# Latent attention with its score blocks in reverse order and a softmax handed over in three parts

## The reference

```
q = rmsnorm(c_q) @ w_q_b          # 128 plain + 64 rotary columns a head
kv = rmsnorm(c_kv) @ w_kv_b       # 128 key + 128 value columns a head
sc = (q_nope . k_nope + q_rope . k_rope) * 192 ** -0.5
p  = softmax(where(key_pos <= q_pos, sc, -1e30))    # blocks of 128 queries
y  = p @ v
```

## Time and profile before

| | |
|---|---|
| median of 3 runs | 2827.41 us (2825.73 to 2827.95) |
| profiled execution | 2832.14 us |
| its span | 2830.3 us, mean granted clock of TensorE 0.988 |
| TensorE busy | 2750.7 us, 97% of the span |
| VectorE / ScalarE / GpSimd busy | 1307.0 / 999.7 / 1069.2 us |

### The profile page before, as it was taken

How to read it: one execution, slowest core, us unless ns; L and a number is a source line. 1 busy time by engine, 2 the same in 40 slices (tenths; PEclk the granted TensorE clock), 3 DMA queues, 4 the chain that set the end, 5 groups by cost and what they waited for, 6 DMA issues and landing times.

```text
span 2830.3 us, 33382 instructions
## 1 busy us (share of the span) xinstructions
PE 2750.7 (97%) x13100; PEld 2283.2 (81%) x13100; DVE 1307.0 (46%) x1887; ACT 999.7 (35%) x1566; POOL 1069.2 (38%) x528
## 2 busy tenths in 40 slices
PE   8999998899999999889999999999999999999997
PEld 7888887788888888777878888888878888888886
DVE  6466647823255665683334555453343222222323
ACT  5235435423224443453342333233223333333221
POOL 1443332244444333223443333333434444444442
PEclk9999998999999999999999999999999999999998
DMA  6422231245434223123542222222223333336333
GB/s 181 137 77 78 72 120 39 57 129 147 119 97 123 80 77 119 40 58 104 152 125 82 75 68 83 79 75 81 89 79 119 112 112 112 112 112 216 112 127 112
DMA packets 307611, 289.13 MB, mean 102 GB/s; under 512 B 33152, under 2 KB 256000, under 8 KB 306944
## 3 DMA queue, kind: packets, MB, share of 16 engines
q1 hardware_dynamic: 300512, 264.40, 31.4%
q10 hardware_dynamic: 6944, 22.61, 2.1%
HBM read 260.19 MB, written 26.74 MB: 101 GB/s over the span
## 4 chain that ended last, share of the span: by engine, by line
PE 81%; DVE 13%; DMA 2%; ACT 2%; issue 1%; POOL 0%; SPq 0%; DVEq 0%; ACTq 0%
PE bank L858 24%; PE bank L860 24%; PE bank L859 24%; DMA w_raw<-in_w_in 1%; PE work L1116 1%; DVE pt L1716 1%; DVE probs L1682 1%; DVE mixed L1460 1%; DVE stat L1675 1%; PE work L972 1%; PE work L974 1%; DMA latent_scr<-mixed 1%; PE o_bank L859 1%; PE o_bank L860 1%; PE o_bank L858 1%
## 5 line engine op out<-in xcount | busy, mean ns | idle before, releaser
L849 POOL TENSOR_TENSOR w_lo<-w_raw,w_hi 128x1024 fp32r<-128x1024 f32 (+3 forms) x460 | 983.8, 2142 | 1472.7 <-ACT w_hi L697 1472.7
L858 PE MATMUL bank<-act_in,w_hi 128*128 128x512 f32 x2662 | 1055.5, 397 | 14.2 <-DVE act_in L1428 11.3
L860 PE MATMUL bank<-act_in,w_lo 128*128 128x512 f32 x2662 | 1041.9, 391 | 0.0
L859 PE MATMUL bank<-act_in,w_hi 128*128 128x512 f32 x2662 | 1040.5, 391 | 0.0
L697 ACT ACTIVATE w_hi<-w_raw 128x1024 fp32r<-128x1024 f32 (+3 forms) x468 | 437.9, 938 | 1057.6 <-PE bank L860 650.1
L858 PEld LDWEIGHTS bank<-act_in,w_hi 128*128 128x128 f32 x2662 | 502.0, 189 | 120.6 <-DVE act_in L1428 14.5
L860 PEld LDWEIGHTS bank<-act_in,w_lo 128*128 128x128 f32 x2662 | 501.3, 188 | 107.6
L859 PEld LDWEIGHTS bank<-act_in,w_hi 128*128 128x128 f32 x2662 | 502.3, 189 | 99.3 <-issue 1.7
L858 PE MATMUL bank<-mixed,w_hi 128*128 128x512 f32 x768 | 299.4, 390 | 0.0
L860 PE MATMUL bank<-mixed,w_lo 128*128 128x512 f32 x768 | 298.8, 389 | 0.0
L859 PE MATMUL bank<-mixed,w_hi 128*128 128x512 f32 x768 | 298.8, 389 | 0.0
(11 more groups left out here) (267 smaller groups left out, 2756.2 us busy)
## 6 DMA issues: line engine op xcount, KB each, us to landing
w_raw<-in_w_in SPq DMA_DIRECT2D x512, 128.0 KB, 2.5
w_raw<-in_w_in SPq DMA_DIRECT2D x224, 256.0 KB, 2.9
w_raw<-in_w_out SPq DMA_DIRECT2D x64, 512.0 KB, 3.7
w_raw<-in_w_in SPq DMA_DIRECT2D x32, 512.0 KB, 3.7
w_raw<-in_w_out SPq DMA_DIRECT2D x64, 256.0 KB, 4.6
x_scr<-buf ACTq DMA_DIRECT2D x32, 256.0 KB, 3.1
probs<-x_scr SPq DMA_DIRECT2D x32, 256.0 KB, 4.9
w_raw<-in_w_attn_up SPq DMA_DIRECT2D x32, 256.0 KB, 2.9
```

The source lines that it names most:

```text
L849: nc.gpsimd.tensor_tensor(lo, raw, hi, ALU.subtract).then_inc(lo_ready, 1)
L858: pe.matmul(dst, lhs[0], rhs[0], start=start, stop=False, skip_group_check=skip)
L859: pe.matmul(dst, lhs[0], rhs[1], start=False, stop=False, skip_group_check=skip)
L860: return pe.matmul(dst, lhs[1], rhs[0], start=False, stop=stop, skip_group_check=skip)
```

## The change

TensorE computes the score blocks in the order 3, 2, 1, 0. `MLA_ORDER` has three parts: block 3, block 2, and blocks 1 and 0. `scored` is raised at the end of each part (still three times a head). VectorE's maxima, ScalarE's exponentials and VectorE's normalizing each go part by part, with one L1676, one crossing to ScalarE, one crossing back and one reciprocal for each part. Where the head before is a latent head too, TensorE starts block 3 when two of its three subtractions are done, and waits for the third ahead of block 1, which is the first that writes `work[0]`. All steps keep their places in the list.

```
+MLA_ORDER = ((3,), (2,), (1, 0))
...
@@ ScalarE
                 elif name == "mla_scores":
-                    asked()
-                    for i in range(NB):
...
+                    for blocks in MLA_ORDER:
+                        asked()
+                        for i in blocks:
+                            at, w = SCORE_AT["mla"][i], P * (i + 1)
+                            ins = act.activation(probs[:, at:at + w], score_bank("mla", i), ACT.Exp,
+                                                 bias=stat[:, 1, i:i + 1], scale=MLA_SCALE,
+                                                 accum_out=stat[:, 2, i:i + 1])
+                        ins.then_inc(from_act, 1)
...
@@ TensorE
+            def after_mla(h):
+
+                return h["kind"] == "mla" and heads[h["j"] - 1]["kind"] == "mla"
...
-                    pe.wait_ge(pt_lo, h["turn0"])
+                    pe.wait_ge(pt_lo, h["turn0"] - after_mla(h))
...
-                    for i in {"mla_scores": range(NB), "sb_scores": range(3), "sb_scores2": (3,)}[name]:
+                    for i in {"mla_scores": range(NB)[::-1], "sb_scores": range(3), "sb_scores2": (3,)}[name]:
...
+                        if i == 1 and after_mla(h):
+                            pe.wait_ge(pt_lo, h["turn0"])
...
-                        if i:
+                        if i != (0 if sbk else 1):
                             ins.then_inc(scored, 1)
...
@@ VectorE
                 elif name == "mla_scores":
                     h = heads[step[1]]
-                    for i in range(NB):
-                        v.wait_ge(scored, h["score0"] + max(1, i))
-                        link(v.tensor_reduce(stat[:, 0, i:i + 1], score_bank("mla", i), AX_X, ALU.max))
-                    ask(v.tensor_scalar(stat[:, 1, :], stat[:, 0, :], -MLA_SCALE, None, ALU.mult))
+                    for n, blocks in enumerate(MLA_ORDER):
+                        v.wait_ge(scored, h["score0"] + n + 1)
+                        for i in blocks:
+                            ins = v.tensor_reduce(stat[:, 0, i:i + 1], score_bank("mla", i), AX_X, ALU.max)
+                        link(ins)
+                        cols = slice(blocks[-1], blocks[0] + 1)
+                        ask(v.tensor_scalar(stat[:, 1, cols], stat[:, 0, cols], -MLA_SCALE, None, ALU.mult))
                 elif name == "mla_norm":
-                    answer()
-                    link(v.reciprocal(stat[:, 5, :], stat[:, 2, :]))
-                    for i in range(NB):
...
+                    for blocks in MLA_ORDER:
+                        answer()
+                        cols = slice(blocks[-1], blocks[0] + 1)
+                        link(v.reciprocal(stat[:, 5, cols], stat[:, 2, cols]))
+                        for i in blocks:
+                            at, w = SCORE_AT["mla"][i], P * (i + 1)
+                            ins = v.tensor_scalar(probs[:, at:at + w], probs[:, at:at + w], stat[:, 5, i:i + 1], None,
+                                                  ALU.mult)
                     ins.then_inc(probs_ready, 1)
```

More of the change, by code:

```diff
@@ L1672, in _ @@
                     h = heads[step[1]]
-                    for i in range(NB):
-                        v.wait_ge(scored, h["score0"] + max(1, i))
-                        link(v.tensor_reduce(stat[:, 0, i:i + 1], score_bank("mla", i), AX_X, ALU.max))
-                    ask(v.tensor_scalar(stat[:, 1, :], stat[:, 0, :], -MLA_SCALE, None, ALU.mult))
-                elif name == "mla_norm":
-                    answer()
-                    link(v.reciprocal(stat[:, 5, :], stat[:, 2, :]))
-                    for i in range(NB):
-                        at, w = SCORE_AT["mla"][i], P * (i + 1)
-                        ins = v.tensor_scalar(probs[:, at:at + w], probs[:, at:at + w], stat[:, 5, i:i + 1], None,
-                                              ALU.mult)
+                    for n, blocks in enumerate(MLA_ORDER):
[5 more added lines that the diff above has]
+                        ask(v.tensor_scalar(stat[:, 1, cols], stat[:, 0, cols], -MLA_SCALE, None, ALU.mult))
+                elif name == "mla_norm":
+                    for blocks in MLA_ORDER:
[6 more added lines that the diff above has]
+                                                  ALU.mult)
                     ins.then_inc(probs_ready, 1)
```

## The result

The changed kernel takes 2836.76 us (median of 5 runs, 2835.97 to 2838.97), the kernel before 2827.41 (5 runs, 2824.05 to 2829.50). The ratio is 1.0037 with a 95% interval of 1.0022 to 1.0052: slower by 9.35 us where 1.4 us less was forecast. The chance given to this side was 0.07, and the range ended at 2830.5.

What follows compares the result with a forecast made beforehand. VectorE with ScalarE's answer was taken to set the pace from head 3 on. Earlier scores and hidden exponentials, less added instructions, gave about 0.7 us a layer, 1.4 in both: 2827.41 to 2826.0 us, range 2821 to 2830.5.

Steps and rivals of the forecast that it cites:

- the sum's bounds: A head's four added small VectorE instructions cost 0.32 to 0.82 us: 2824.8 to 2828.8 us in all.
- the term: Normalizing on VectorE: widest product first may save up to 0.5 us a head; taken at nothing, lower end to 2823.5.
- Instructions and their price: VectorE's two more L1676 and two more reciprocals: 0.47 us a head, counted in heads 1, 3, 4 and 5.
- the rule weighed: Skill text on VectorE: each added instruction costs its own length, 0.70 us a head instead of 0.47; not followed.
- The early start: TensorE's scores start after two of three subtractions, 0.41 us earlier; VectorE sets the pace from head 3 on.
- ScalarE's wait gone: VectorE's wait for ScalarE's exponentials, 5.4 us a layer, falls to near nothing; 0.78 us won in an even head.
- rival 1: Half-clock scores of head 1 speed up, 3.2 us a layer: 2819.6 us, or 2822.8 in one layer only; chance 0.16.
- signs of being wrong: Head 1's scores take about 3.8 us, a reciprocal delays the next product over 0.25 us, or L1716 waits longer.
- Rival 3: Handovers between VectorE and ScalarE, three times a head, cost more than they hide: slower; chance 0.08.
- Rival 2: TensorE carries the chain, so each of 14 score starts gives 0.41 us: 2821.5 us; chance 0.08.

Runs made afterwards that it cites:

- changed again: The changed kernel timed once more with no edit, for a second profile: 2836.46 us, ratio 1.003 to the kernel before.
- first experiment: The changed kernel with scores and exponentials still in three parts but normalized in one (one reciprocal, four products, block 3 last): 2819.80 us, ratio 0.998.
- last experiment: The kernel before with two more reciprocals ahead of the norm's products, their order kept: 2832.94 us, ratio 1.002.
- the order alone: The changed kernel with only block order and early start kept; maxima and exponentials ask and answer once, norm as before: 2825.14 us, ratio 0.9998.

## Why the prediction was wrong

| kernel, and what it is compared to | difference in norm sum | difference in time |
|---|---|---|
| two reciprocals more, to before | 6.4 | 6.0 |
| three-part norm, to before | 10.8 | 11.1 |
| changed, to normalized in one | 16.7 | 15.8 |
| changed again, to normalized in one | 14.2 | 16.0 |
| split held, to normalized in one | 4.7 | 5.2 |
| small products on ScalarE, to normalized in one | 22.5 | 25.8 |
| normalized in one and held, to normalized in one | -0.1 | 0.9 |
| no early start, to normalized in one | 1.2 | 2.3 |
| widest first, to normalized in one | 4.2 | 7.3 |
| three reciprocals, widest last, to normalized in one | 8.3 | 11.4 |
| before with the split held, to before | -0.4 | 4.2 |

(Us; times are differences of E: 9.35 + 6.5, 9.5 + 6.5, for the changed kernel.) The last three rows don't follow the sum; see "Left open". Of the changed kernel against before, the norm sum is 16.7 us more and the rest of the change brings 6.5 us (first experiment): 10.2 us, where 9.35 were measured.

**The step that failed.** It is this sentence of the sum's bounds: "In some heads the four products take 1.80 us where the lengths by shape, less the overlap, allow 1.3; with the widest first this may fall by up to 0.5 us a head, which I take at nothing and which lowers the lower end". The half microsecond was seen and not followed to its cause, which was the split of 256 columns on GpSimd, and the term had the wrong sign: nothing in the sum stands for a product of VectorE that waits for GpSimd. The norm is 2.1 us longer in heads 0, 2 and 4. Of this the two reciprocals, which the sum has, are 0.4, so the term measures +1.7 us (head 0 gets half of the 2.1 back, as before the large split met its gate product). In head 6 it is a split in front of two products, 4.54 us in place of 0.55, of which much is given back: before, the same splits hit the gate's product and cast (1.36 and 2.50 us, now 0.69 and 0.43), so from reciprocal to subtraction the head is 9.37 - 7.73 = 1.64 us longer. The reader can see the fault in what I read: the earlier trace rows are the timeline of VectorE alone. Of the 15.8 us by which the changed kernel is slower than the same with a norm in one, the held split gives back 10.6. The remaining terms stand up: without the three-part norm the change brings 6.5 us, with an interval of 3.1 to 7.9, and the sum without its reciprocals (0.42 us less cost in eight to ten heads) makes 4.8 to 5.6.

**Instructions and their price.** Right in size, wrong in place. There are 64 instructions more. In head 3 the maxima run from 485.47 to the next instruction at 487.65, 2.18 us; before they took 2.17, and 2.23 was forecast.

```profile
485.47 0.69 DVE L1685 TENSOR_REDUCE stat<-work 128x1 f32<-128x512 f32 x1
486.20 0.15 DVE L1688 TENSOR_SCALAR stat<-stat 128x1 f32<-128x1 f32 x1
486.27 0.55 DVE L1685 TENSOR_REDUCE stat<-work 128x1 f32<-128x384 f32 x1
...
487.57 0.17 DVE L1688 TENSOR_SCALAR stat<-stat 128x2 f32<-128x2 f32 x1
487.65 0.68 DVE L1424 TENSOR_TENSOR probs<-bank,cos 128x512 f32<-128x512 f32 x1
```

Two reciprocals more in a head without a split: head 7, 1.87 - 1.49 = 0.38 us, forecast 0.42. Together 0.39 us of the 0.47; the rule weighed would have made it 0.70, so the rows decide for themselves here. The sum counts them in heads 1, 3, 4 and 5 alone, which for the reciprocals is 8 x 0.42 = 3.4 us. The last experiment has 6.0 (3.1 to 7.9), and the held split leaves 5.2 over the norm in one. Both look more like all heads, but neither excludes 3.4.

**The early start.** Of the right size, not shown beyond the noise. The sum has 0.41 us at the scores of heads 1, 2 and 7, in both layers 2.5 us; the experiment has 2.3, with overlapping intervals. The wait ahead of the scores fell by 6.2 us, though, more than the 2 to 4 forecast, because the norm takes over as the place where TensorE waits.

**ScalarE's wait gone.** Right, from 5.4 us in the first stretch to nothing, and the chain through head 4 is without ScalarE. With a norm in one, parts in the scores bring 5.3 us over the order alone.

**The rivals.** What rival 1 describes happened, and with it one of the signs of being wrong: the scores of head 1 run at a granted clock of 1.00, 2.4 GHz, in both layers, and take 3.74 us where they took 6.93 in the first:

```profile
451.60:455.40 3.80, 3.80 (x26) 3.56 (x26) 2.82 (x6) 2.15 (x5) 0.29 (x1) 1.00 0.13 37
1174.10:1178.20 4.10, 4.10 (x27) 3.78 (x26) 3.15 (x7) 2.46 (x5) 0.29 (x1) 1.00 0.11 32
```

It won nothing that can be seen, since 1.2 GHz came back behind other waits: the mean granted clock of the stretches is 0.94 and 0.92, against 0.93 and 0.94. Rival 3 had the right side by a wrong mechanism, dear handovers. From the end of the last exponential to the start of the reciprocal the trace of before has 0.03 us (head 2, 481.47 and 481.50), and three crossings each way with the norm in one gave the fastest kernel of all. Rival 2 isn't seen, as the chain stays on VectorE.

**Left open.** Why the kernel before with the split held has the low clock more often. And why the time of two kernels (widest first, three reciprocals with the widest last) grows by some 3 us more than the norm sum. The clock may be part of it: their mean granted clock is 0.989 and 0.990 (0.9889 and 0.9895), that of the first experiment 0.991 (0.9908), and among the 33 runs of before 0.001 of it goes with 1.7 us. That makes an estimate of 3.2 and 2.2 us, from a correlation and not from a test.

## What to carry to other kernels

Before adding or moving small work on VectorE, lay its timeline beside GpSimd's. Here an fp32 product or cast from SBUF to SBUF that started just behind a GpSimd split lasted until that one's end. The profile shows it as a long duration, never as a wait; 0.4 us of delay cost 2 to 4 here. Put the handovers where VectorE reads PSUM (the maxima), keep what comes last ahead of a waiting engine in as few instructions as can be, and don't expect that holding GpSimd back removes the collision: it may only move to the next product or cast, as in head 6.

## What the runs showed of the hardware

- A GpSimd subtraction of 768 columns (1.80 us) held back a product of 128 columns until its end. That is a wait for the other's whole instruction, not a shared rate. The other way round, the split of 256 columns took 1.03 us in place of 0.73 when a product was ahead of it.
- VectorE's reads with one input in PSUM ran through a split in 1.51 us for two, and take 1.52 where none runs.
- Among instructions on SBUF alone the kind decides. In the trace of the changed kernel 14 maxima of 128 columns of `probs` (L1666) started inside a split and took 0.28 to 0.29 us, as outside one, and reciprocals kept their 0.15 to 0.18. Casts of 512 columns (L1206, 0.90 to 2.23 us in place of 0.43), products with a column of `stat` (L1696, of 128 columns up to 2.36 in place of 0.28) and additions of two SBUF tiles (L1262, 2.48 us in place of 0.69) were held back.
- A recorded start doesn't tell who is first. A product of 128 columns recorded up to 0.03 us ahead of the split was held back for all of it; in the last experiment products of 512 columns with a lead of 0.08 us were not, and the split of 768 took 2.08 us in place of 1.80.
- A program without any edit of order can come out either way at such a meeting: a norm of 2.15 or 4.05 us in the same profile, by 0.3 us of earlier history.
